# One core, two-layer encoder trunk: the first mixer, its projections and their adaLN rows in one line of 48 units

## The reference, cut to what matters

```python
u = x * (1.0 + sc1) + sh1
y = even_mixer(u, ...) if l == 0 else odd_mixer(u, ...)
x = layer_norm(ALPHA * x + (1.0 + g1) * y, ln_g[l, 0], ln_b[l, 0])
u = x * (1.0 + sc2) + sh2
y = conv_ffn(u, ...)            # up 2048 x 11008, causal conv of 3, gelu * a, down 5504 x 2048
x = layer_norm(ALPHA * x + (1.0 + g2) * y, ln_g[l, 1], ln_b[l, 1])
```

## Time and profile before, and how to read it

| | |
|---|---|
| median of 3 runs | 2500.13 us (2499.15 to 2501.19) |
| the profiled execution | 2498.65 us |
| its span, first to last instruction | 2496.9 us |
| mean granted TensorE clock | 0.952 |
| TensorE, VectorE, ScalarE busy | 91%, 70%, 41% |
| moved by DMA | 612.28 MB, mean 245 GB/s |

### The profile page before, as it was taken

The page is one execution under the profiler, slowest core; times in us unless marked ns, Lnnn a source line. Parts: engine busy times, 40 slices in busy tenths (PEclk is TensorE's granted clock), DMA queues, the critical chain, the costliest instruction groups (busy, mean ns, idle before and its releaser), DMA issues.

```text
span 2496.9 us, 29787 instructions
## 1 busy us (share of the span) xinstructions
PE 2263.6 (91%) x10289; PEld 1871.4 (75%) x10289; DVE 1753.9 (70%) x1948; ACT 1019.5 (41%) x1005; POOL 1.2 (0%) x5
## 2 busy tenths in 40 slices
PE   1479966989999999999988999987999999999996
PEld 1368754868888888888866888876888888888885
DVE  5876787878886767776767887786878655555455
ACT  0243331345554344444343444423555433444432
POOL 0000000000000000000000000000000000000000
PEclk9689977989999999999989999998999999999998
DMA  7989786857877777786748888795677556555553
GB/s 273 325 302 313 239 278 207 310 206 252 294 247 243 259 260 266 259 294 223 258 173 289 297 281 292 256 340 174 225 271 278 186 193 202 186 185 186 165 193 130
DMA packets 407845, 612.28 MB, mean 245 GB/s; under 512 B 20868, under 2 KB 204860, under 8 KB 405964
## 3 DMA queue, kind: packets, MB, share of 16 engines
q1 hardware_dynamic: 407756, 611.13, 71.8%
HBM read 608.96 MB, written 2.10 MB: 245 GB/s over the span
## 4 chain that ended last, share of the span: by engine, by line
PE 82%; DVE 9%; DMA 4%; ACT 2%; issue 2%; SPq 1%; DVEq 0%; ACTq 0%
PE bank L1197 26%; PE bank L1199 26%; PE bank L1206 25%; DMA ada_w<-in_w_ada 3%; DVE ada_acc L324 2%; PE bank L1270 2%; DVE ada_acc_gla L324 1%; DVE w_lo L777 1%; ACT w_hi L514 1%; DVE ada_acc_start L324 1%; PE bank L1230 1%; PE bank L1227 1%; ACT u_f L666 0%; PE bank L1217 0%; DVE ada_acc_alt L324 0%
## 5 line engine op out<-in xcount | busy, mean ns | idle before, releaser
L777 DVE TENSOR_TENSOR w_lo<-w_raw,w_hi 128x2048 fp32r<-128x2048 f32 x380 | 846.1, 2233 | 485.2 <-ACT w_hi L514 419.0
L514 ACT ACTIVATE w_hi<-w_raw 128x2048 fp32r<-128x2048 f32 x380 | 709.9, 1870 | 932.8 <-PE bank L1199 809.0
L1197 PE MATMUL bank<-w_hi,u_hi 128*128 128x512 f32 (+1 forms) x2176 | 861.0, 397 | 0.9 <-DVE u_lo L848 0.9
L1199 PE MATMUL bank<-w_hi,u_lo 128*128 128x512 f32 (+1 forms) x2176 | 845.8, 390 | 0.0
L1206 PE MATMUL bank<-w_lo,u_hi 128*128 128x512 f32 (+1 forms) x2176 | 532.0, 387 | 9.2 <-DVE w_lo L777 9.2
L1197 PEld LDWEIGHTS bank<-w_hi,u_hi 128*128 128x128 f32 x2176 | 414.3, 190 | 88.1 <-issue 3.6
L1199 PEld LDWEIGHTS bank<-w_hi,u_lo 128*128 128x128 f32 x2176 | 414.2, 190 | 85.2 <-issue 3.4
L1206 PEld LDWEIGHTS bank<-w_lo,u_hi 128*128 128x128 f32 x2176 | 405.3, 188 | 92.3 <-DVE w_lo L777 9.6
L324 DVE SCALAR_TENSOR_TENSOR ada_acc<-ada_w,silu_c,ada_acc 128x512 f32<-128x512 f32 x510 | 382.7, 750 | 21.3 <-DMA ada_w<-in_w_ada 2.2
L1197 PE MATMUL bank<-w_hi,hid_hi 128*128 128x512 f32 x688 | 270.1, 393 | 0.0
L1199 PE MATMUL bank<-w_hi,hid_lo 128*128 128x512 f32 x688 | 269.2, 391 | 0.0
(11 more groups left out here) (183 smaller groups left out, 1285.4 us busy)
## 6 DMA issues: line engine op xcount, KB each, us to landing
ada_w<-in_w_ada SPq DMA_DIRECT2D x384, 512.0 KB, 5.7
w_raw<-in_w_up SPq DMA_DIRECT2D x344, 512.0 KB, 5.4
w_raw<-in_w_down SPq DMA_DIRECT2D x152, 512.0 KB, 4.6
w_raw<-in_w_qkv SPq DMA_DIRECT2D x96, 512.0 KB, 4.8
w_raw<-in_w_in_ab SPq DMA_DIRECT2D x64, 512.0 KB, 6.3
w_raw<-in_w_out_ab SPq DMA_DIRECT2D x32, 512.0 KB, 6.9
w_raw<-in_w_o SPq DMA_DIRECT2D x32, 512.0 KB, 5.0
w_raw<-in_w_down SPq DMA_DIRECT2D x40, 256.0 KB, 3.9
```

The lines of the kernel that those rows point to most:

```text
L514: nc.scalar.activation(whi[:, u % HL_SLOTS, 0:width], raw[:, u % RAW_SLOTS, 0:width], ACT.Copy).then_inc(w_hi, 1)
L777: nc.vector.tensor_tensor(wlo[:, u % HL_SLOTS, 0:width], raw[:, u % RAW_SLOTS, 0:width], whi[:, u % HL_SLOTS, 0:width].bitcast(f32), ALU.s ...
L1197: nc.tensor.matmul(banks[t][:, 0:width], h_at(kt, t), w, start=first and n == 0, stop=False)
L1199: ins = nc.tensor.matmul(banks[t][:, 0:width], l_at(kt, t), w, start=False, stop=False)
```

## The change

The 32 units of the in-projection and the 16 of the out-projection become one list. Its order (IN_ORDER) needs only the first two groups of channels of u for 16 units: a chunk's groups 0 and 1 are added up, ScalarE copies the half sum to z and the bank is free; later TensorE puts it back into a bank by a matmul with the identity (f32, 128 x 512, one per half of the frames) and adds groups 2 and 3 (units 16 to 31). adaLN blocks become 24 pairs of 128 x 1024 (shift with scale, or two halves of a gate), a row tile per DMA of 512 KB; ada_plan gives each unit the rows beside it: one pair before unit 0, nine beside the 48 units, fourteen after. The mixer's parts are put behind single units: low-rank gate at 17 and 18, its map at 19, the heads' transposes and decays at 21 to 24, pooling at 26 to 29, the heads' scores, states and values at 30 to 34, the scaling by ScalarE (before: VectorE) at 35, transposes at 36 and 37. The low-rank product is 48 matmuls with 256 columns instead of 96 with 16, and b_gate is a 17th row of its map. The heads go one at a time through banks 4, 5 and 7. x is loaded in four parts, b_ada through ScalarE's queue, and the other row tensors through GpSimd's, due at unit 11. All loops are written out, so that registers go. The output tail stands ahead of the last low half of its chunk, and at three layer norms that low half goes behind the fourth low piece of u (hold, after). Constants are split in two tensors, and small tensors move in memory.

The diff, cut to its core:

```diff
+Q, K, V0, V1, R0, R1, P0, P1 = 2, 3, 4, 5, 6, 7, 0, 1
+IN_ORDER = [(Q, 0), (K, 0), (V0, 0), (Q, 1), (K, 1), (V0, 1)]
+IN_ORDER += [(c, g) for c in (V1, R0, R1, P0, P1) for g in (0, 1)]
+IN_ORDER += [(Q, 2), (K, 2), (Q, 3), (K, 3)]
+IN_ORDER += [(c, g) for c in (R0, R1, P0, P1, V0, V1) for g in (2, 3)]
+PART_CHUNKS = [Q, K, V0, V1, R0, R1, P0, P1]
+PART_BANKS = {c: 2 * (n % 3) for n, c in enumerate(PART_CHUNKS[:6])} | {P0: 0, P1: 2}
+PART_SLOT = {IN_ORDER.index((c, 1)): n for n, c in enumerate(PART_CHUNKS)}
+FULL_CHUNKS = [Q, K, R0, R1, P0, P1, V0, V1]
+FULL_BANKS = {c: 2 * (n % 2) for n, c in enumerate(FULL_CHUNKS)}
+FULL_SLOT = {IN_ORDER.index((c, 3)): n for n, c in enumerate(FULL_CHUNKS)}
+IN_UNITS, FRONT_UNITS = 32, 48
+OUT_ORDER = [(c, j) for c in (0, 1, 2) for j in (0, 1)] + [(c, j) for c in (0, 1, 2) for j in (2, 3)]
+OUT_ORDER += [(3, j) for j in range(4)]
+OUT_BANKS = (0, 2, 4, 0)
+OUT_LAST = {IN_UNITS + OUT_ORDER.index((c, 3)): c for c in range(4)}
+LR_SLOT, GATE_SLOT = 17, 19
+HEAD_S1 = {21 + h: h for h in range(GH)}
+HEAD_S2 = {30 + h: h for h in range(GH)}
+HEAD_S3 = {31 + h: h for h in range(GH)}
+POOL_MEAN = {26: (0, 1), 28: (2, 3)}
+POOL_MAP = {27: (0, 1), 29: (2, 3)}
+Y_B_T = {36: (4, 5), 37: (6, 7)}
...
+ADA_PAIRS = [(0, 0, g) for g in range(4)] + [(0, 2, n) for n in range(2)] + [(0, 3, g) for g in range(4)]
+ADA_PAIRS += [(0, 5, n) for n in range(2)] + [(1, 0, g) for g in range(4)] + [(1, 3, g) for g in range(2)]
+ADA_PAIRS += [(1, 2, n) for n in range(2)] + [(1, 3, g) for g in (2, 3)] + [(1, 5, n) for n in range(2)]
...
+    def fill(m, first, counts):
+        left = [(m + k, r) for k in range(sum(counts) // KT) for r in range(KT)]
+        for s, n in enumerate(counts):
+            at[first + s] = at.get(first + s, []) + left[:n]
+            left = left[n:]
+        assert not left
+    fill(1, -1, [4] * 4)
+    fill(2, 3, [3, 3, 3, 3, 2, 2])
+    fill(3, 9, [3, 3, 3, 3, 2, 2])
+    fill(4, 15, [3, 3, 3, 3, 3, 3, 3, 4, 3, 3, 3, 4, 3, 4, 3])
+    fill(7, 30, [2, 1, 2, 2, 3, 5, 4, 4, 4, 2, 4, 2, 4, 2, 4, 3])
...
+    first = PH[0, "down_a"]["unit"] + 1
+    fill(12, first, [2] * 8)
+    fill(13, first + 10, [2] * 8)
...
+    ends = {m: max(s for s in at if (m, KT - 1) in at[s]) for m in range(1, len(ADA_PAIRS))}
+    ends[1], ends[7] = 1, 38
...
+            def load_row(m, r):
+                layer, part, n = ADA_PAIRS[m]
+                sp.wait_ge(a_step, m * KT + r + 1)
+                w = A["w_ada"][layer].rearrange("(k p) (s n c) -> p k s n c", p=P, s=6, n=4)
+                w = w[:, r, part, 2 * n:2 * n + 2, :] if part in (2, 5) else w[:, r, part:part + 2, n, :]
+                sp.dma_start(ada_w[:, r % ADA_SLOTS, :].rearrange("p (b c) -> p b c", b=2), w
+                             ).then_inc(a_loaded[r % ADA_SLOTS], 16)
+            def load_unit(u, halves):
+                sp.wait_ge(w_lo, u + 1)
                 for dst, src in halves(raw[:, u % RAW_SLOTS, :]):
                     sp.dma_start(dst, src).then_inc(w_loaded[u % RAW_SLOTS], 16)
+                for s in range(-1, 3) if u == 3 else (u - RAW_SLOTS,) if u >= 7 else ():
+                    for m, r in ADA_ROWS.get(s, ()):
+                        load_row(m, r)
...
+            for r in range(KT):
+                load_row(0, r)
+                if r == 3:
+                    load_x(0)
...
+            for v in range(FRONT_UNITS):
+                if v == 3:
+                    load_x(1)
+                c, j = IN_ORDER[v] if v < IN_UNITS else OUT_ORDER[v - IN_UNITS]
+                load_quarter(v, w_in if v < IN_UNITS else w_out, c, j)
+                if v in (6, 8):
+                    load_x(2 + (v == 8))
+                if v == 9:
+                    gate_load(0, 2, 0)
...
+            sp.wait_ge(sem("gla_o"), GH)
...
+            for s in range(FRONT_UNITS):
+                if s == 2:
+                    for v in (2, 3):
+                        x_piece(v)
+                    for v in (2, 3):
+                        u_piece(v)
+                hi_unit(s + 2)
+                if s in PART_SLOT:
+                    n = PART_SLOT[s]
+                    c = PART_CHUNKS[n]
+                    act.wait_ge(w_used, s + 1)
+                    for t in range(NT):
+                        ins = nc.scalar.activation(z[:, t, c * NCOL:(c + 1) * NCOL], bank[PART_BANKS[c] + t][:, :],
...
+            def ada_row(m, r):
+                acc, w = acc_of(m), ada_w[:, r % ADA_SLOTS, :]
+                dve.wait_ge(a_loaded[r % ADA_SLOTS], 16 * (m * (KT // ADA_SLOTS) + r // ADA_SLOTS + 1))
+                if r == 0:
+                    nc.vector.tensor_scalar(acc[:, :], w, silu_c[:, 0:1], None, ALU.mult).then_inc(a_step, 1)
+                else:
+                    dve.wait_ge(a_step, m * KT + A0 + r)
+                    nc.vector.scalar_tensor_tensor(acc[:, :], w, silu_c[:, r:r + 1], acc[:, :],
+                                                   ALU.mult, ALU.add).then_inc(a_step, 1)
...
                     for j in range(2, own + 2):
+                        if tail and j == own + 1:
+                            tail(c)
+                        if (j < own or more or c != hi - 1) and not (hold and c == hi - 1 and j == own + 1):
+                            lo_unit(unit_no(key, c, j), ph["kts"][j] * NCOL if j < own else UNIT)
...
+                    if v == 3:
+                        lo_unit(after)
...
+                if s in OUT_LAST:
+                    out_tail(OUT_LAST[s])
+                if s < FRONT_UNITS - 1:
+                    lo_unit(s + 2)
...
+            for u in range(FRONT_UNITS):
+                if u < IN_UNITS:
+                    c, j = IN_ORDER[u]
+                    b = PART_BANKS[c] if j < 2 else FULL_BANKS[c]
+                    first, last, after = j == 0, j % 2 == 1, 2 + U_FIRST + 2 * j + 2
...
+                    if j == 2:
...
+                        pe.wait_ge(sem("z_part"), PART_CHUNKS.index(c) + 1)
+                        for t in range(NT):
+                            nc.tensor.matmul(bank[b + t][:, :], ident, z[:, t, c * NCOL:(c + 1) * NCOL],
+                                             start=True, stop=False)
+                else:
+                    c, j = OUT_ORDER[u - IN_UNITS]
+                    b = OUT_BANKS[c]
+                    first, last, after = j == 0, j == 3, 2 + U_MIX + 2 * j + 2
...
+                unit(u, [(k, 4 * j + k) for k in range(4)], (uhi, ulo), first, last, bank[b:b + 2], after)
...
-            chunks((0, "in"), 2, 4)
-            chunks((0, "in"), 4, 8)
```

More of the change, by code:

```diff
@@ L53, in plan @@
         if layer % 2 == 0:
-            phases += [(layer, "in", 8, four, 3), (layer, "mix", 0, four, 7), (layer, "out", 4, four, 2)]
+            phases += [(layer, "in", 8, four), (layer, "out", 4, four)]
         else:
[L56 to L65, removed]
+            phases += [(layer, "qkv", 12, four), (layer, "o", 4, four)]
+        phases += [(layer, "up_a", FT_A // 2, four), (layer, "down_a", 4, (4, 4, 4, 4, 2, 2)),
+                   (layer, "up_b", FT_B // 2 + 1, four), (layer, "down_b", 4, (4, 4, 4, 4, 4, 3))]
@@ L528, in body @@
                         if j == 2 and mid:
-                            mid(c0, i)
+                            mid(c)
                     if tail:
-                        tail(c0, i)
-                if hi - lo == 1 or not more:
-                    for c in range(lo, hi):
-                        body(c, 0)
-                else:
-                    pairs(act, lo, hi, body)
-            def chunk_end(key, c0, i):
-                ph = PH[key]
-                own = 2 if key[1] == "up_b" and c0 == 11 else ph["n"]
-                act.wait_ge(w_used, unit_no(ph, c0, i, own)[1])
@@ L814, in steps, with beside @@
-            def steps(key, lo, hi, mid=None, tail=None, more=True, norm=None):
+                    at = 96 * layer + KT * part + 4 * n
+                    nc.vector.tensor_tensor(mod[:, at:at + 4], ada_p[:, 0:4], cols[:, at:at + 4], ALU.add)
+                    at += KT
+                    nc.vector.scalar_tensor_tensor(mod[:, at:at + 4], ada_p[:, 4:8], 1.0, cols[:, at:at + 4],
+                                                   ALU.add, ALU.add).then_inc(a_out, 1)
+            def beside(s):
+                for m, k in ADA_SUMS.get(s, ()):
+                    ada_evac(m, k)
+                for m, r in ADA_ROWS.get(s, ()):
+                    ada_row(m, r)
@@ L825, in body @@
                         if j == 2 and mid:
-                            mid(c0, i)
-                        if norm is not None and c0 == lo and i == 0:
+                            mid(c)
+                        if norm is not None and c == lo:
                             ln_affine(norm, j - 2)
-                        if beside:
-                            blk, row = beside
-                            row += sum(now[:j - 2])
-                            ada_rows(dve, nc.vector, ada_acc, blk[3], row, row + now[j - 2])
@@ L833, in body @@
```

(13 more changed lines are left out.)

1165 lines of the change are left out of this document (521 added, 644 removed).

## The result

The changed kernel takes 2460.67 us, median of 4 runs (2459.12 to 2461.89), against 2500.17 for the kernel before: a ratio of 0.984, 95% interval 0.9825 to 0.9859. It is faster by 39.5 us, or 1.6%; 100 us were forecast, and 2460.67 lies above the range of 2365 to 2440.

The account below looks back on a forecast made before the run. TensorE, busy 91% of the span but unevenly, was taken as the bound, with the front rewritten. Line -80, layer norms -6, attention -16 and down_a +2 took 2498.65 to 2399 us; range 2380 to 2425, with rivals 2365 to 2440.

Parts of the forecast that it names:

- adaLN sums 10: Line of 48 units: x transposes and adaLN sums together take 10 us of TensorE's 332 us of work.
- VectorE falls 1.2 + 2.3 + 3.7 = 7 us behind: Down_a of layer 0, chunk ends: VectorE's lag makes low halves about 1 us late twice, +2 us, ends 0 and 4.
- The slower rival: Line: TensorE's small gaps lower its clock, 5.4 us more per step, 2637 if in all; chance 0.05 for over 2505.
- The line, -80 forecast: Front of 48 units, in- and out-projection with mixer: unit 47 ends at 440 instead of 520.1 us.
- step s: Line: VectorE's low half of unit s+2, then the rows of s, beside unit s+1; the larger work counts.
- three groups of steps: Line: steps 3 to 16, 17 to 29 and 30 to 46, forecast at 91, 112 and 143 us, 346 in all.
- an allowance of 14: Line: waits through three engines (log-sigmoid chain 4, heads 4, square root and scaling 2, rows 44 and 45 4), 14 us.
- The prediction's sign for the queue: Line: VectorE waiting more than 20 us for ada_w would show the forecast wrong, with the queue as cause.
- the rival that the queue binds everywhere: Line: at 325 GB/s the steps take 380 us instead of 346, giving 2433 us; chance 0.14.
- The identity matmuls: Line, TensorE: 16 matmuls putting half sums back, 0.9 us each, 14 us, ends 4 and 19; covered except in steps 17 to 29.
- The third rival: Mixer in the line: each head's chain through three engines stops the units; about 2450 us; chance 0.10.
- Layer norms and attention: Three layer norms lose 6 us as a low half moves; attention stage loses 16, range 5 to 20, from fewer waits.

Follow-up runs that it names:

- run 346: Not a run's label: "in any run 346" gives a queue rate, 346 GB/s, the best stage of over 90 us in any of the runs.
- the last experiment: GpSimd's 14 small row tensors after pair 0, x's first quarter behind row 11, against the kernel with sums, gate and pool loads later and rows forward: 2395.05 us.

## Why the prediction was wrong, point by point

- **The step that failed: a sum's place in TensorE's order.** Moving the sums of pairs 4 to 17, 22 and 23 one slot on took off 48.9 us in all, and 36 of the 38 by which the two down and two up_a stages were too long. The forecast priced a sum by its matmuls only ("adaLN sums 10") and took each step as the larger of VectorE's and TensorE's work. It asked what VectorE's debt does to the next low half, not to the sum, which stands nearer. "VectorE falls 1.2 + 2.3 + 3.7 = 7 us behind, and a low half comes about 1 us late at each of two ends" has a debt and names the wrong waiter: in down_a TensorE never waited for a low half, and 7.2 us for the last rows of two sums. Measured: +17.9 there, +14.0 in down_b, which the forecast passed over though it gets two pairs in the same way, +4.2 in each up_a (a wait of 1.9 and a slower unit behind it). With the sums one slot later these became +3.2, +2.6 and -0.6. The evidence was in the earlier trace rows: 5.9 and 4.4 us were exactly such waits, and the forecast used them only as waits that would go.
- **The clock behind a wait.** Down_a's waits are 7.2 us and its loss by them 14.8. The slower rival looked at the low clock as a state of the line. Granted were 0.94 from unit 3 to unit 46 and 0.89 in units 4 to 16, behind waits at sums; a line held at the low level did not come about. The forecast counted the low clock at units 0 and 3 and as 5 us behind the waits that were to go from the attention stage, and nothing for it behind the waits of its own line and stages.
- **The line, -80 forecast, -53.3 measured.** Unit 0 began at 43.8, not 36: pair 0's rows ended at 34.5 instead of 27.5, as the rows' bytes and others came at 337 GB/s where a row each 1.34 us asks for 391, and the sum took 3.57, not 1.84: it has eight column sums where a block had four, and the earlier trace rows has 1.84 for four. Unit 3 began at 84.2, not 72.7, and ended at 91.7, not 80.5. The forecast's step s runs beside unit s+1, so its three groups of steps are units 4 to 17, 18 to 30 and 31 to 47:

```profile
91.70:203.70 112.00, 94.75 (x407) 76.22 (x406) 81.78 (x63) 43.91 (x48) 0.00 (x0) 0.89 0.91 330
203.70:313.70 110.00, 110.00 (x510) 85.91 (x509) 91.67 (x81) 54.30 (x67) 0.00 (x0) 1.00 0.94 333
313.70:466.80 153.10, 128.22 (x568) 101.00 (x567) 126.81 (x147) 43.85 (x42) 0.00 (x0) 0.90 0.79 282
```

They took 112.0 against 91, 110.0 against 112 and 153.1 against 143, beside an allowance of 14. With the start these are 11, 21, -2 and 10 us less the 14, which is 26 of the 27 missing. The whole miss of the line thus lies ahead of unit 18: in the start, and in units 4 to 17, where TensorE waited 10.1 and 5.1 us at the sums of pairs 2 and 3 and the mean clock was 0.89. From there on the forecast was even 6 us too long. That is luck in part: TensorE waited 10.0 us at units 38 and 39 for the low halves of the mixer's last pieces, 4.0 and 10.8 at sums, and no sum's wait was among the allowances.
- **The queue's rate.** "The fastest stretch moved 409 GB/s" was a burst of 17 us; units 3 to 46 moved 318 at a DMA share of 0.89, and the best stage of over 90 us in any run 346. Such averages are no limit of the queue either. Inside units 4 to 16 it moved 293 GB/s for 34 us and 407 for 26 (a share above 1 says that a short window is read some 4% too high):

```profile
91.00:125.00 34.00, 32.65 (x149) 26.95 (x148) 25.80 (x17) 15.45 (x16) 0.00 (x0) 1.00 0.84 293
...
170.00:196.00 26.00, 20.95 (x84) 16.39 (x83) 16.70 (x15) 9.42 (x11) 0.00 (x0) 0.87 1.04 407
```

SyncE issues in order, and from 91 to 196 us it waited 56.8 us itself for VectorE to free a slot for a row. The rows of units 4 to 16 were late by this order and by the bytes ahead of them; for the first pair the last experiment says so only weakly, and the rest was not held up by bytes. The prediction's sign for the queue, VectorE waiting more than 20 us for rows in the line, came true with 36.0 us, 5.6 of them ahead of the very first row. Still the rival that the queue binds everywhere, at 2433, was too broad: from unit 17 on halved bytes changed little (267.4 us to the line's end against 270.3). The Trainium skill (DMA: Bandwidth & Descriptors, "Where 436 GB/s comes from") puts the HBM side at about 358 GB/s; the long stretches here (94 us and more) average below it, at 318 to 346, one of 27 us reached 359, and the 26 us above and the earlier trace rows pass it, at 407 and 409, so as a limit it does not hold here. Taken by its estimate, 15 us more, the line would have been forecast at 455.
- **The identity matmuls** (16 of them, 14 us forecast): 16.6 busy in the trace, no wait before them. The copies by ScalarE cost nothing of their own. Units 18 to 30, where both stand with gate, heads and pooling, came 2 us below the forecast's 112. From 196.5 to 371 us, where the heads' parts stand, TensorE waited for nothing; only the mixer's last pieces stopped it, for the 10.0 us at units 38 and 39. The third rival, that each head's chain stops the units, is so refuted, and that its time of 2450 was the nearest to the result is luck.
- **VectorE's wide row**: 1.28 busy, as forecast.
- **Layer norms and attention**: -5.9 and -18.3 against -6 and -16. TensorE's waits in the attention stage answer to the earlier trace rows: of 9.2, 5.9 and 4.4 there remain 6.4 at the burst and 3.1 at the last pair's sum.

```profile
PE bank L1130 <- DVE w_lo L737: 6.4, 1, 6.4
PE bank L1143 <- DVE ada_acc L747: 3.1, 1, 3.1
```

- **Unrolled loops**: full stages are not longer (up_b 264.6 us against 266.5, the rest of layer 1 502.8 against 502.7), so instruction fetch cost nothing that shows.

Why unit 3 begins 11.5 us late in the kernel after can be read from its trace. It inherits 7.8 from unit 0. VectorE's chain of four low halves and the 16 rows of pair 1 ran from 43.75 to 75.95, 32.2 us where 30.7 were forecast, with 2.1 us of waits for rows in it. The sum at the lower level and two pieces of u took 8.2 us to the start of unit 3, not 6. Halved bytes took 1 us off the 29.8 from unit 2's end to unit 3's, halved accumulation 5. Open is whether another order of those rows and low halves would start unit 3 sooner; no version of it was run. The wait before unit 38 was halved, not removed.

## What to carry to other kernels

When an engine that runs in order gets a small step that reads another engine's result, ask where that result stands in the other engine's order, and put the step one slot behind it: here two changed lines gave 49 us, more than the whole change had gained. Then look whether the wait is gone or has moved: in the down stages it was gone, in the line a part of it came back at a low half. Price a short wait in a full stage with the lower clock that follows it, about as much again. And take a queue's rate neither from its best burst nor as one figure: look at what stands ahead of the urgent loads and whether the issuing engine waits itself, and move what is not yet due behind what is.

## What the runs showed that I had not expected

A short wait in a full stage cost about twice its length. Against the kernel with the sums later, waits of 7.2 us in down_a made 14.8 us, 5.9 in down_b made 11.3, and 1.9 in up_a made 4.8. In down_a the two units behind the waits ran at granted clocks of 0.50 and 0.65, and the same eight column sums took 1.95 us at full clock and 3.57 at the lower level. It is no rule for longer waits in a stage with slack: in the line 4.0 and 10.8 us gave back 12.4, layer norm 0 counted in. The queue's rate follows the engines as much as it leads them: with the same bytes, down_a showed 286 GB/s when TensorE stood at its sums and 323 when it did not.
